# Retention decay tables as products of two exponentials made one head ahead, and linear-mixing queries scored in a 128-row contraction

## What is computed

```python
proj = rms_norm(x, ln_mix_pre[l]) @ w_in[l]
c_q, c_kv, k_pe, conv_u, r_q, r_k, r_v, r_g, gate_logits = jnp.split(proj, points, axis=-1)
y_mla = mla_branch(...); y_conv = conv_branch(...); y_ret = retention_branch(...)
merged = gates[:, :, 0] * y_mla + gates[:, :, 1] * y_conv + gates[:, :, 2] * y_ret
x = x + rms_norm(merged @ w_out[l], ln_mix_post[l])
x = x + rms_norm(ffn(rms_norm(x, ln_ffn_pre[l])), ln_ffn_post[l])
```

```python
q_pe = apply_rope(q[..., 64:96], cos, sin); k_pe = apply_rope(k_pe, cos, sin)
s = einsum('bqhd,bkhd->bhqk', q_nope, k_nope) + einsum('bqhr,bkr->bhqk', q_pe, k_pe)
```

```python
scores[i, j] = q[i] . k[j] * (gamma_f ** (i - j) if i >= j else gamma_b ** (j - i))
o = scores @ v
```

## Time and profile before

| what | us |
|---|---|
| median of 3 runs | 3031.52 |
| lowest, highest | 3027.76, 3033.35 |
| the profiled execution | 3027.72 |
| its span | 3025.9 |
| TensorE busy in it | 2853.0 |
| layer 0, layer 1 of the second block (about) | 978 to 2008, 2008 to 3026 |

### The profile page before, as it was taken

How to read it: one execution, slowest core, us unless ns; L and a number is a source line. 1 busy time by engine, 2 the same in 40 slices (tenths; PEclk the granted TensorE clock), 3 DMA queues, 4 the chain that set the end, 5 groups by cost and what they waited for, 6 DMA issues and landing times.

```text
span 3025.9 us, 33780 instructions
## 1 busy us (share of the span) xinstructions
PE 2853.0 (94%) x13324; PEld 2239.2 (74%) x13324; DVE 1335.2 (44%) x1719; ACT 1201.0 (40%) x1737; POOL 1224.1 (40%) x555
## 2 busy tenths in 40 slices
PE   8997899899999899999998999979998999899997
PEld 4776677678888676677786888857766877778885
DVE  5656432431112778644515202268776263341123
ACT  5346653342223555333334222254544233433222
POOL 1122233344445463343444444435624434344442
PEclk9998999999999999999999999989999999999998
DMA  6333222232223211122231222221111212222221
GB/s 236 108 123 122 74 84 80 95 121 97 98 98 112 98 64 39 54 89 77 84 125 70 98 98 97 98 98 70 63 36 70 94 73 98 91 98 98 91 98 63
DMA packets 89373, 278.08 MB, mean 92 GB/s; under 512 B 10048, under 2 KB 10240, under 8 KB 89216
## 3 DMA queue, kind: packets, MB, share of 16 engines
q1 hardware_dynamic: 89216, 275.92, 25.3%
HBM read 268.54 MB, written 7.34 MB: 91 GB/s over the span
## 4 chain that ended last, share of the span: by engine, by line
PE 75%; DVE 15%; ACT 6%; issue 2%; DMA 1%; POOL 1%; SPq 0%; DVEq 0%; ACTq 0%; POOLq 0%
PE bank L1426 22%; PE bank L1427 22%; PE bank L1428 22%; PE bank L1662 2%; DVE pageF L2363 2%; PE bank L1477 1%; PE bank L1612 1%; DVE pageF L2441 1%; DVE pageF L2437 1%; ACT L1707 1%; DVE smal L2136 1%; PE bank L1624 1%; DVE pageR L2236 1%; PE bank L1653 1%; DVE pageF L2171 1%
## 5 line engine op out<-in xcount | busy, mean ns | idle before, releaser
L2473 POOL TENSOR_TENSOR wlo<-wraw,whi 128x1024 fp32r<-128x1024 f32 x429 | 1049.9, 2449 | 1515.9 <-ACT whi L1690 1501.5
L1426 PE MATMUL bank<-pageR,whi 128*128 128x512 f32 x3552 | 1443.2, 406 | 73.5 <-ACT pageR L1849 27.4
L1427 PE MATMUL bank<-pageR,whi 128*128 128x512 f32 x3552 | 1383.6, 390 | 0.0
L1428 PE MATMUL bank<-pageR,wlo 128*128 128x512 f32 x3552 | 1383.3, 389 | 0.0
L1426 PEld LDWEIGHTS bank<-pageR,whi 128*128 128x128 f32 x3552 | 675.6, 190 | 255.0 <-issue 106.4
L1427 PEld LDWEIGHTS bank<-pageR,whi 128*128 128x128 f32 x3552 | 676.1, 190 | 151.5 <-issue 23.8
L1428 PEld LDWEIGHTS bank<-pageR,wlo 128*128 128x128 f32 x3552 | 674.7, 190 | 140.3
L1690 ACT ACTIVATE whi<-wraw 128x1024 fp32r<-128x1024 f32 x429 | 450.9, 1053 | 395.9 <-PE bank L1428 392.4
L1730 ACT ACTIVATE pageR<-pageF 128x512 fp32r<-128x512 f32 x136 | 85.9, 632 | 445.0 <-DVE pageF L2230 208.2
L2363 DVE SCALAR_TENSOR_TENSOR pageF<-pageF,prm 128x497 f32<-128x497 f32 (+9 forms) x180 | 205.1, 1140 | 2.5
L2482 POOL TENSOR_TENSOR pageR<-pageF,pageR 128x512 fp32r<-128x512 f32 x46 | 66.7, 1463 | 150.2 <-ACT pageR L1730 138.0
(11 more groups left out here) (200 smaller groups left out, 2116.7 us busy)
## 6 DMA issues: line engine op xcount, KB each, us to landing
wraw<-in_wst SPq DMA_DIRECT2D x429, 512.0 KB, 3.5
pageF<-in_wmod SPq DMA_DIRECT2D x96, 256.0 KB, 5.0
pageF<-in_xT SPq DMA_DIRECT2D x16, 256.0 KB, 4.4
pageF<-in_bias SPq DMA_DIRECT2D x16, 256.0 KB, 4.2
kept<-pageF SPq DMA_DIRECT2D x16, 256.0 KB, 4.8
pageF<-kept SPq DMA_DIRECT2D x16, 256.0 KB, 4.2
pageF<-tables SPq DMA_DIRECT2D x8, 256.0 KB, 4.5
out_x<-pageF SPq DMA_DIRECT2D x8, 256.0 KB, 2.0
```

The costliest lines, as they stand in the source:

```text
L1426: e.matmul(o, hi, xh, start=first, stop=False)
L1427: e.matmul(o, hi, xl, start=False, stop=False)
L1428: i = e.matmul(o, lo, xh, start=False, stop=last)
L2473: e.tensor_tensor(wlo[:, b % NH, :, :], wraw[:, b % NR, :, :], bc(whi[:, b % NH, :, :]), ALU.subtract).then_inc(*wlod.up(("wlo", b)))
```

## The change

Queries: the projection's rows 64 to 127 are multiplied by one page `rotm` that holds the cosine on rows 64 to 95 and the sine on rows 96 to 127, in one DVE operation on 64 partitions. The sum of the two products is left to the score matmul, which now contracts over all 128 rows: `rope_kpe` puts the turned key on rows 64 to 95 and, by one more copy, on rows 96 to 127. The keys of heads 4 to 7 reuse the pages of heads 0 to 3, whose rows 64 to 127 stay as they are; only four heads are copied.

Decay: for a head ACT takes exp(lb*rA2) in two halves of 448 columns into two pages `tE` and exp(lf*rA1) into `tabD`, and DVE multiplies the one into the other. Head 0's table is planned when `side_ret` begins, before `ready`; head h+1's behind the scores of head h. The step and yield that stood ahead of the scores are gone.

```diff
 def main_mla():
-    for name in ("cosm", "sinm", "cosr", "sinr"):
+    for name in ("rotm", "cosr", "sinr"):
 ...
 # make(j)
-    pages.take(("ks", l, 2 * j + hp))
+    if j < 2:
+        pages.take(("ks", l, 2 * j + hp))
 ...
     pages.take(("qs", l, h))
-    pages.take(("rq", ("qs", l, h)))
     step("mla_q", l, h)
-    pages.give(("rq", ("qs", l, h)), ("qpe", l, h))
 ...
+def ret_decay(h):
+    for i in range(2):
+        pages.take(("tE", l, h, i))
+    step("ret_decay", l, h)
+    for i in range(2):
+        pages.give(("tE", l, h, i), ("tD", l, h))
+
 def side_ret():
+    ret_decay(0)
     for h in range(4):
         yield from p.ready(("rg", l, h, 1))
-        step("ret_decay", l, h)
-        yield
         for j in range(4):
 ...
         pages.give(("rk", l, h), ("rs", l, h, 3))
+        if h < 3:
+            ret_decay(h + 1)
         for i in range(2):
 ...
 # sync, load_table("rotm")
+    rows = slice(64 + 32 * i, 96 + 32 * i)
+    load(F((name, l))[rows, :], tables[i][rows, :], part + "m", l)
 ...
 # tensor, mla_scores
-    e.matmul(bank(job), F(("qs", l, h))[0:96, 128 * qt:128 * qt + 128], F(("ks", l, h))[0:96, :],
+    e.matmul(bank(job), F(("qs", l, h))[:, 128 * qt:128 * qt + 128], F(("ks", l, h % 4)),
 ...
 # scalar, ret_decay
-    w.wait_ge(*when("tDl", l, h))
-    e.activation(tabD[:, :], tabD[:, :], ACT.Exp).then_inc(*fun.up(("tD", l, h)))
+    for i in range(2):
+        clear(("tE", l, h, i))
+        e.activation(F(("tE", l, h, i))[:, 0:448], rA2[:, 448 * i:448 * i + 448], ACT.Exp,
+                     scale=lb).then_inc(*fun.up(("tE", l, h, i)))
+    if l or h:
+        w.wait_ge(*(when("ra", l, h - 1, 3) if h else when("ra", l - 1, 3, 3)))
+    e.activation(tabD[:, :], rA1, ACT.Exp, scale=lf).then_inc(*fun.up(("tDf", l, h)))
 ...
 # vector, mla_q (was rope96: three operations)
+    e.tensor_tensor(F(("qs", l, h))[64:128, :], bank(o)[64:128, :], F(("rotm", l))[64:128, :],
+                    ALU.mult).then_inc(*vec.up(("qpe", l, h)))
 ...
 # vector, mla_k
-    e.tensor_copy(F(("ks", l, h))[64:96, :], F(("kpe", l))[64:96, :])
+    if j < 2:
+        e.tensor_copy(F(("ks", l, h))[64:128, :], F(("kpe", l))[64:128, :])
 ...
 # vector, rope_kpe
+    e.tensor_copy(d[96:128, :], d[64:96, :]).then_inc(*vec.up(("kpe", l)))
 ...
 # vector, ret_decay
-    e.tensor_scalar(tabD[:, :], rA1, lf, None, ALU.mult).then_inc(*vec.up())
-    after()
-    e.scalar_tensor_tensor(tabD[:, :], rA2, lb, tabD[:, :], ALU.mult, ALU.add).then_inc(
-        *vec.up(("tDl", l, h)))
+    w.wait_ge(*when("tDf", l, h))
+    for i in range(2):
+        t = tabD[:, 448 * i:448 * i + 448]
+        w.wait_ge(*when("tE", l, h, i))
+        e.tensor_tensor(t, t, F(("tE", l, h, i))[:, 0:448], ALU.mult).then_inc(*vec.up(("tD", l, h)))
```

More of the change, by code:

```diff
@@ L990, in after @@
                     over = ("av", "mla", l, j, qt)
-                    for k in (("ks", l, 2 * j), ("ks", l, 2 * j + 1), ("qs", l, 2 * j), ("qs", l, 2 * j + 1),
-                              ("mv", l, j)):
+                    for k in (("qs", l, 2 * j), ("qs", l, 2 * j + 1), ("mv", l, j)):
                         pages.give(k, over)
+                    if j >= 2:
+                        for hp in range(2):
+                            pages.give(("ks", l, 2 * j - 4 + hp), over)
                     live.discard(j)
@@ L1002, in maker @@
                 p.drop(xkv, ("o", "w_v" + L, 3))
-                for name in ("cosm", "sinm"):
-                    pages.give((name, l), ("qpe", l, 7))
-                pages.give(("kpe", l), ("kpd", l, 7))
+                pages.give(("rotm", l), ("qpe", l, 7))
+                pages.give(("kpe", l), ("kpd", l, 3))
             def scores(job):
```

55 lines of the change are left out of this document (32 added, 23 removed).

## The result

The changed kernel takes 3019.06 us at the median (3013.45 to 3020.17, 6 runs), the kernel before 3031.17 us (3027.76 to 3033.35, 6 runs): ratio 0.9961, 95% interval [0.9951, 0.9971]. It is faster by 12 us, where 26 were forecast, and lies 0.06 us outside the forecast range. That the median fell just outside and not just inside is within the spread of the six runs; that half of the gain is missing is not. The profiled execution has a span of 3011.7 us, 14.2 us less than before.

The account below looks back on a forecast made before the run. TensorE, busy 94% of the span, was taken as the bound, so only its waits count. Gains of 12.5 us in layer 0 and 13.8 in layer 1, together 26.3, gave a forecast median of 3005 us, range 2997 to 3019.

Parts of the forecast that it names:

- Term A: Early decay table: head 1's wait for products and slow passes shrink, worth 5.6 us in layer 0, 6.1 in layer 1.
- Rival 3: Weight splits, on ACT behind the next head's Exp and both evictions, starve TensorE; slower, 3050 us; chance 0.04.
- Term B: Queries: one DVE operation instead of three shortens the waits for the query copy, worth 5.5 and 6.3 us per layer.
- Score matmuls and key copies: Scores over 128 rows in place of 96, and changed turned-key copies where TensorE does not wait on DVE: zero.
- Term C: One gate projection planned into the tail of latent attention as filler; counted 0, bounds 0 and 1.0 us per layer.
- Term D: Last retention head: wait for its low halves shrinks by 1.4 us per layer, bounds 0 and 2.0.
- Rival 1: The wait moves to head 0's late table and head 1's crowded DVE queue; Term A lost, 3017 us; chance 0.14.

Follow-up runs that it names:

- e3: The changed kernel with the pause of one filler group ahead of each head's scores put back; 3011.75 us, ratio 0.9946.
- e4: The changed kernel with a planner rule: a weight split due between a head's first retention product and its squares is planned behind the squares; 3004.29 us, ratio 0.9920.
- f8: e4 with the same rule also around the convolution's silus; instruction order came out as e4's; 3006.71 us, ratio 0.9926.
- g12: e4's kernel run again in the third series; 3007.44 us, ratio 0.9924.
- f5: The changed kernel with the table made in the old way, at the new place behind the scores of the head ahead; 3014.35 us, ratio 0.9951.
- f6: The changed kernel with the new table form at the old place, with the pause before the scores; 3025.87 us, ratio 0.9987.
- g10: f5 (old table form at the new place) with the held-split rule of e4; 3005.85 us, ratio 0.9915.
- e1: The kernel before with the query part alone, decay table made as before; 3022.48 us, ratio 0.9980.

## Why the prediction was wrong

**Term A, the table: mechanism right, one step failed.** At head 1 the wait of 4.95 us became 1.52, and the passes gave 5.26-3.96 = 1.3 us back (5.72-3.96 = 1.8 in layer 1): 4.7 and 5.2 us, where 5.6 and 6.1 were forecast. In head 0, where I took 0.5 us, there is no wait. The step that failed is what the lost pause does to ACT's order. The prediction counts the pause only as time, TensorE coming one filler group sooner, and says of ACT "That costs these evictions nothing". It does cost the evictions nothing, but I never asked what comes to stand ahead of the squares behind them. With one filler group fewer the next split falls behind the second eviction; with the pause back, and the table as early, it does not (e3). Rival 3 names the split that now stands behind both evictions and asks whether the split is late for TensorE; it is not, no wait for a weight appears. What is late is what the split stands in front of: the squares. The excerpt of ACT's order on record ends with that split, one row ahead of the squares. Priced from rows of before, the split's 1.05 us and a two-input DVE operation that lasts until POOL's subtraction is over (2.72 us) would make a norm 2 to 3 us late wherever this order comes up (an estimate), which is in three heads of four in both layers. (How the 10 us divide between the split on ACT and POOL's part of it on DVE no run separates: holding the split back removes both.) e4 against the changed kernel gives the sum: 10.3 us in the stretches, and 11.5 us by the ratios (0.9961-0.9923, the mean of e4, f8 and g12, of 3030 us).

The table's early place was thus the reason for the gain, and the lost pause that came with it the reason for the loss. f5, f6 and g10 settle that the other half of this part, the product of two exponentials, gave nothing: at the new place the old form takes 4.0 us of DVE and is as fast, at the old place the new form doesn't help.

The Trainium skill (SBUF — State Buffer, "SBUF: two separate sides") was weighed in the prediction, at the wrong instructions. The two multiplications of head 0 met a split and took 1.74 us, those of head 1 met none and took 1.15: 0.6 us, where up to 2 were feared, and TensorE didn't wait. The place where its rule cost time is L1972: 2.04 us with a subtraction on POOL beside it, 0.69 without (both rows above), its end 0.54 us behind POOL's. With that rule the trace agrees there.

**Term B, the queries: right.** Forecast 5.5 and 6.3 us, measured 5.0 and 5.9; with other starts 4.4 to 5.0 and 5.7 to 7.5 in the nine further profiles that have them. The residual wait was 0.75 us (forecast 0.5), and no slow steps stand behind it. The split was out of the way, as I argued.

**Score matmuls and key copies.** L1628 takes 601 ns with 128 rows, 603 with 96: right. The copy added to `rope_kpe` was put at zero, since TensorE was said not to wait on DVE there. It costs 0.45 us in layer 0, as shown above, and 0.35 to 0.47 in layer 1: most of the 1.0 us by which the queries' stretch fell short.

**Term C, the moved filler: size wrong, and it depends on the rest.** I counted 0 with bounds of 0 and 1.0 us of gain. In e1, with the pause in its old place, the tail to norm lost 3.5 us, with two new waits of 1.0 us a layer in it. In the changed kernel, where the pause is gone, they don't appear. If these waits are its price, which no run separates, a bound with the other sign was missing.

**Term D, the last head: right by itself, eaten.** The wait for the halves fell by 2.0-0.6 = 1.4 us, exactly the term. But the norms of heads 2 and 3 wait for their squares, 0.63 and 1.14 us, and the stretch lost 0.6 us. In e4, without the split ahead, it gains 1.7 us a layer.

**The clock behind old waits.** TensorE waits 2.17 us for L2236 of before (L2263 of the changed kernel) behind the layer's norm, and 2.13 to 2.18 us there in all 14 traces. Busy time by stretch in the 6 us from there (columns as above, the clock third from the end), in the changed kernel:

```profile
1621.00:1627.00 6.00, 5.94 (x19) 4.76 (x20) 1.35 (x2) 3.70 (x5) 4.36 (x2) 0.72 0.13 35
```

in e4:

```profile
1617.30:1623.30 6.00, 5.94 (x25) 4.81 (x26) 1.35 (x2) 3.71 (x5) 4.35 (x2) 1.00 0.12 31
```

and in the kernel before:

```profile
1630.20:1636.20 6.00, 5.90 (x25) 4.81 (x26) 1.35 (x2) 3.75 (x5) 4.31 (x2) 1.00 0.13 31
```

The same wait in front of the same matmuls leaves the clock at 1.00 in one program and takes it to a mean of 0.72 in the other, part of it at 1.2 GHz: 25 matmuls in 6 us or 19. The changed kernel lost time by it in both layers; the stretch is 1.8 and 1.6 us longer. I had no term for that, and it is not the change's: e4, f8 and g12 are one program, and their stretch "next" costs 0.2, 3.3 and 3.3 us.

One thing in the traces goes with it. TensorE waits once more some 8 us ahead of this wait (1.08 us in layer 0 of the kernel before, 0.21 us in the changed kernel). Over both layers of the 14 traces that earlier wait is 0.76 us or less in 15 cases, and in all 15 the matmuls behind the later wait take 1.5 to 1.6 us longer; it is 0.85 us or more in the other 13, and there they do so once (e3, layer 0). The earlier wait is short where TensorE comes to it late, up to 0.8 us behind the kernel before, and in the changed kernel it had then run slower further ahead, behind a wait of 9.33 us: in the 6 us behind that wait the granted clock was 0.53, and 0.67 in the kernel before. So one fall of the clock goes together with the next; that it causes it is not shown.

**The size of noise.** The start, up to 955 us, has the same operations in the same order in all these programs, with other page numbers only. The first 955 us in f5:

```profile
0.00:955.00 955.00, 891.02 (x4569) 703.32 (x4570) 367.00 (x538) 399.46 (x597) 322.26 (x140) 0.97 0.33 111
```

and in g12:

```profile
0.00:955.00 955.00, 888.68 (x4533) 699.70 (x4534) 366.00 (x535) 397.20 (x594) 314.90 (x137) 0.96 0.32 110
```

f5 is 36 matmuls ahead, 8 us. One profiled execution can mislead by that much. The stretches behind the start mislead less: in e4, f8 and g12, one program, they differ by 0.7, 1.0 and 0.0 us, and by 3.1 in "next".

**Rivals.** None of them happened as written. Rival 1's number is near the result (3017), but not its mechanism: the table's wait did not move to head 0's table or head 1's queue; the queue of head 1 is crowded by the norm that the split made late (1.52 us, 0.45 with the split held). Rival 3 had the right instruction and asked the wrong question of it.

**What holds of the forecast.** With the split held, e4, f8 and g12 give 3004.3, 3006.7 and 3007.4 us, a gain of 24.7, 23.8 and 23.1; the forecast was 3005, a gain of 26.3. Its terms were the terms of that program, which has a rule that the changed kernel lacks.

## What to carry to other kernels

When an instruction is moved in an in-order queue, or a pause is taken out so that others move, list for each what it now stands in front of, row by row, down to the first instruction that another engine waits for, and not only what it stands behind and who needs its own result. Work that has slack (here a weight split, three blocks ahead) belongs behind work that has none, and a planner that places it by a count of steps should be told so. Before making a computation cheaper, try it at the other place alone: of the decay part's gain the place was worth all, the form none.

## What was not expected of the hardware

- A DVE operation with one SBUF input is held by POOL as well, which the prediction's pricing of two-input operations left out. In f5 L2429 (TENSOR_SCALAR, 128x896) takes 0.68 us for head 0 and 2.87 us for head 2, where it starts together with a subtraction on POOL and ends 0.48 us behind it:

```profile
1201.56 0.68 DVE L2429 TENSOR_SCALAR tabD<-tabA,smal 128x896 f32<-128x896 f32 x1
```

```profile
1239.88 2.39 POOL L2493 TENSOR_TENSOR wlo<-wraw,whi 128x1024 fp32r<-128x1024 f32 x1 [2.92 <-ACT whi L1702]
```

- Waits are worth more than their length: 7.0 us less idle made the stretches 10.3 us shorter (e4 against the changed kernel).
- The same 2.17 us wait is followed by 0 or 1.6 us of slower matmuls. The same operations in the same order ran 8.6 us apart over the first 955 us (start -3.7 in f5, +4.9 in g12), and one and the same program 6.5 us apart (-1.6 in e4, +4.9 in g12).
